# The end of a two-block transformer kernel: squares and statistic of one token half moved one step ahead, one activation table for both roots, three residual pairs added by TensorE

## The reference, cut to what matters

```python
    h2 = _rmsnorm(x, g_mlp_pre[l])
    ff = jnp.einsum('bsf,fd->bsd',
                    jnp.square(jax.nn.relu(jnp.einsum('bsd,df->bsf', h2, w_up[l]))), w_down[l])
    x = x + _rmsnorm(ff, g_mlp_post[l])
```

## Time and profile before

| | us |
|---|---|
| median of 3 runs | 2459.04 (2458.66 to 2460.85) |
| the profiled execution | 2458.39 |
| its span | 2456.7 |
| TensorE busy | 2421.7 (99%) |
| VectorE busy | 1678.2 (68%) |
| ScalarE busy | 1050.0 (43%) |
| last product of step 27 begins | 2432.38 |
| last addition on VectorE ends | 2452.87 |

### The profile page before, as it was taken

One profiled execution on the slowest core, in us unless ns is written; L12 is line 12 of the kernel. 1 busy time (PEld: TensorE's weight loads), 2 busy tenths in 40 slices (PEclk: granted clock), 3 DMA queues, 4 the chain that ended last, 5 costly groups with the idle time before them and its releaser, 6 DMA issues.

```text
span 2456.7 us, 29766 instructions
## 1 busy us (share of the span) xinstructions
PE 2421.7 (99%) x11558; PEld 1928.9 (79%) x11558; DVE 1678.2 (68%) x1992; ACT 1050.0 (43%) x1503; POOL 139.1 (6%) x227
## 2 busy tenths in 40 slices
PE   8999999999999999999999999999999999999997
PEld 6887766688888888888788777788878888888885
DVE  5238776646877778698873655455588877786888
ACT  5225676634433333333642333333356333334336
POOL 1002100000000010000001000000001000100001
PEclk9999999999999999999999999999999999999999
DMA  6110000142433381500134122233445533715103
GB/s 222 50 43 22 2 1 1 53 146 103 155 123 109 103 308 65 209 1 18 53 108 142 43 81 72 72 134 135 143 150 176 172 103 105 262 45 196 45 1 137
DMA packets 76245, 252.22 MB, mean 103 GB/s; under 512 B 6320, under 2 KB 6368, under 8 KB 76080
## 3 DMA queue, kind: packets, MB, share of 16 engines
q1 hardware_dynamic: 43792, 131.08, 16.7%
q0 software_dynamic: 32320, 119.32, 13.0%
HBM read 186.78 MB, written 62.91 MB: 102 GB/s over the span
## 4 chain that ended last, share of the span: by engine, by line
PE 79%; DVE 8%; ACT 2%; issue 2%; DVEq 0%; ACTq 0%
PE ps L2720 24%; PE ps L3133 20%; PE ps L3171 18%; PE ps L3301 6%; PE ps L3004 2%; PE ps L3066 1%; DVE opQ_lo L2135 1%; DVE opQ_lo L2132 1%; PE ps L3046 1%; DVE spot L2177 1%; DVE ql_raw L2172 1%; PE ps L3228 1%; PE ps L3247 1%; PE ps L2968 1%; PE ps L3237 1%
## 5 line engine op out<-in xcount | busy, mean ns | idle before, releaser
L3171 PE MATMUL ps<-opQ_hi 128*128 128x512 f32 x896 | 350.3, 391 | 2.8 <-DVE opQ_lo L2135 2.8
L3171 PE MATMUL ps<-opQ_lo,opQ_hi 128*128 128x512 f32 x896 | 348.8, 389 | 0.0
L3171 PE MATMUL ps<-opQ_hi,opQ_lo 128*128 128x512 f32 x896 | 348.7, 389 | 0.0
L3171 PEld LDWEIGHTS ps<-opQ_hi 128*128 128x128 f32 x896 | 168.2, 188 | 42.1 <-DVE opQ_lo L2135 7.1
L2720 PE MATMUL ps<-opP_hi,w_hi 128*128 128x512 f32 x638 | 199.0, 393 | 2.1 <-DVE T L2419 0.7
L2720 PE MATMUL ps<-opP_lo,w_hi 128*128 128x512 f32 x638 | 196.6, 389 | 0.0
L2720 PE MATMUL ps<-opP_hi,w_lo 128*128 128x512 f32 x638 | 196.4, 389 | 0.0
L3171 PEld LDWEIGHTS ps<-opQ_hi,opQ_lo 128*128 128x128 f32 x896 | 168.2, 188 | 35.2
L3171 PEld LDWEIGHTS ps<-opQ_lo,opQ_hi 128*128 128x128 f32 x896 | 168.2, 188 | 34.6 <-issue 0.2
L1275 ACT ACTIVATE opQ_hi<-spot 128x1024 fp32r<-128x1024 f32 x80 | 84.9, 1061 | 235.8 <-PE ps L3171 196.7
L885 ACT ACTIVATE w_hi<-w_stage 128x1024 fp32r<-128x1024 f32 x104 | 109.3, 1051 | 174.1 <-PE ps L2720 145.7
(11 more groups left out here) (444 smaller groups left out, 4750.9 us busy)
## 6 DMA issues: line engine op xcount, KB each, us to landing
w_stage<-in_w_stream SPq DMA_DIRECT2D x104, 512.0 KB, 3.7
h_spill<-T POOLq DMA_DIRECT2D x56, 512.0 KB, 5.3
pair_raw<-in_w_stream SPq DMA_DIRECT2D x26, 1024.0 KB, 5.8
spot<-in_w_stream SPq DMA_DIRECT2D x24, 1024.0 KB, 7.1
spot<-h_spill POOLq DMA_DIRECT2D x24, 1024.0 KB, 9.5
qh_raw<-in_w_stream SPq DMA_DIRECT2D x8, 1024.0 KB, 11.1
ql_raw<-h_spill POOLq DMA_DIRECT2D x8, 1024.0 KB, 7.5
g_spill<-T POOLq DMA_DIRECT2D x16, 512.0 KB, 2.9
```

The lines of the kernel that those rows point to most:

```text
L3171: mm = pe.matmul(ps[:, down_bank(sc, f) + m, :], weight, operand, start=(g == 0 and kt == 0 and weight is wh and operand is hi), stop=(g = ...
```

## The change

On four engines the order at the end is written anew.

- VectorE and ScalarE: the squares of half 1 and their sums (`end_square`, `end_add`) of tiles 0 to 5 now follow the folds of step 25, ahead of the parts of step 26; tiles 6 and 7 follow those parts. Before, tiles 0 to 3 (VectorE) or 0 to 4 (ScalarE) followed the parts of step 26 and the others those of step 27.
- TensorE: the statistic of half 1 is taken in the middle of step 26 instead of step 27.
- ScalarE: behind the squares of tiles 6 and 7 one table set with both the logarithm and the exponential is loaded (`preload_act_table_set`); the four loads at the roots are gone. Three gains of half 1 come ahead of step 27's parts. The root of half 1 comes behind six gains, ahead of the squares of half 0, and all four squares' gains of half 0 come ahead of the last folds.
- The residual of pair 0 of half 0 is also added by TensorE (`TURNED_PAIRS`): three turned pairs instead of two. The first tile of the first of them now stands ahead of the four squares' products of half 0 on TensorE. All three copies by ScalarE come at its very end, and all three stores go by GpSimd; SyncE stores the other three pairs of half 0.
- VectorE: the scales and the residual additions are two functions now; three scales of half 1 come ahead of the last folds.

```diff
+TURNED_PAIRS = ((1, 0), (1, 1), (0, 0))
...
-            for j in range(3):
-                sp.wait_ge(n4["added"], 2 * DT + 2 + j + 1)
+            for j in range(1, 3):
+                sp.wait_ge(n4["added"], 2 * DT + 2 + j)
                 sp.dma_start(out_pair(0, j), end_pair(X, 0, j)).then_inc(y_stored, 16)
...
-            for j in range(2):
-                pool.wait_ge(n4["ln"], 3 + j + 1)
-                pool.dma_start(out_pair(1, j), end_pair(X, 1, j)).then_inc(ya_stored, 16)
-            pool.wait_ge(ya_stored, 16 * 4)
+            for i, (h, j) in enumerate(TURNED_PAIRS):
+                pool.wait_ge(n4["ln"], 3 + i + 1)
+                pool.dma_start(out_pair(h, j), end_pair(X, h, j)).then_inc(ya_stored, 16)
+            pool.wait_ge(ya_stored, 16 * 5)
...
-                        if sc == 1 and i == 26:
-                            if x == 0:
-                                gate_square(0)
-                                gate_square(1)
-                            else:
-                                for o in range(5):
-                                    end_square(1, o)
+                        if sc == 1 and i == 26 and x == 0:
+                            gate_square(0)
+                            gate_square(1)
+                        if sc == 1 and i == 25 and x == 1:
+                            for o in range(6):
+                                end_square(1, o)
+                        if sc == 1 and i == 26 and x == 1:
+                            end_square(1, 6)
+                            end_square(1, 7)
+                            act.preload_act_table_set("natural_log_exp_and_others")
+                            for o in range(3):
+                                end_gain(1, o)
...
-            for o in range(5, DT):
-                end_square(1, o)
-            for o in range(5):
-                end_gain(1, o)
+            for o in range(3, 6):
+                end_gain(1, o)
+            half_root(n4, 2, 0, end_r[1])
+            for o in range(6, DT):
+                end_gain(1, o)
             for o in range(4):
                 end_square(0, o)
-            half_root(n4, 2, 0, end_r[1])
+            for o in range(4):
+                end_gain(0, o)
             for o in range(4, DT):
                 end_square(0, o)
-            for o in range(5, DT):
-                end_gain(1, o)
             half_root(n5, 2, 1, end_r[0])
-            for o in range(DT):
+            for o in range(4, DT):
                 end_gain(0, o)
-                if o in (1, 5):
-                    pair_out(o // 4)
+            for i in range(3):
+                pair_out(i)
...
+                        if sc and x == 1 and i == 25:
+                            for o in range(6):
+                                end_add(1, o)
                         if sc and i == 26:
                             down_turn(x)
...
-                    for o in range(4):
+                    for o in range(6, DT):
                         end_add(1, o)
...
-            for o in range(4, DT):
-                end_add(1, o)
...
+            end_scale(1, 0)
+            end_scale(1, 1)
             for o in range(4):
                 end_add(0, o)
+            end_scale(1, 2)
             for o in range(4):
                 last_fold(1, o)
-            for j in range(4):
-                end_scale(1, j)
-            for j in range(4):
+            end_scale(1, 3)
+            end_residual(1, 2)
+            end_residual(1, 3)
+            end_scale(0, 0)
+            for j in range(1, 4):
                 end_scale(0, j)
+                end_residual(0, j)
...
-                            if x == 1 and sc == 1 and i == STEPS - 1 and kt == 1:
+                            if x == 1 and sc == 1 and i == STEPS - 2 and kt == 1:
                                 pe.wait_ge(ff["down"], vec_no(1, 1, "F5b"))
                                 half_statistic(n4, 2, 0, mix_sum)
...
+            def turned(i, x):
+
+                h, j = TURNED_PAIRS[i]
+                n = 2 * (2 * (j % 2) + x) + j // 2
+                pe.wait_ge(n4["scaled"], 2 * DT + 4 * (1 - h) + j + 1)
+                pe.wait_ge(tile_landed[n], END_BACK[n])
+                for tiles in (X, Xend):
+                    mm = pe.matmul(ps[:, 2 + 2 * i + x, :], ident[:, :], end_pair(tiles, h, j)[:, x],
+                                   start=(tiles is X), stop=(tiles is Xend))
+                return mm
+
+            turned(0, 0)
             for o in range(4, DT):
                 pe.wait_ge(n5["sq"], 2 * DT + o + 1)
                 mm = pe.matmul(ps[:, 1, :], ones[:, :], end_sq[(o - 1) % 4], start=False, stop=(o == DT - 1))
             mm.then_inc(n5["stat"], 1)
...
+            turned(0, 1).then_inc(n4["stat"], 1)
+            pe.wait_ge(ff["down"], vec_no(1, 1, "F4_3"))
+            for i in range(1, 3):
+                turned(i, 0)
+                turned(i, 1).then_inc(n4["stat"], 1)
```

More of the change, by code:

```diff
@@ L1350, in end_square, with end_gain @@
                 act.activation(dst, X[:, 2 * m + a, cols_of(h)], ACT.Square).then_inc(norm["sq"], 1)
+            def end_gain(h, o):
+                a, m = o // 4, o % 4
+                n = 2 * m + a
+                act.wait_ge((n5, n4)[h]["sq"], 16 + o + 1)
+                act.activation(X[:, n, cols_of(h)], X[:, n, cols_of(h)], ACT.Copy, scale=col[:, C_MLPPOST + n:C_MLPPOST + n + 1])                   .then_inc(n5["hi"], 1)
             for n in range(FF_PLAIN[0]):
@@ L1580, in _, with pair_out @@
             down_act(1)
[L1582 to L1592 removed]
+            def pair_out(i):
+                h, j = TURNED_PAIRS[i]
+                act.wait_ge(n4["stat"], 3 + i + 1)
+                act.activation(end_pair(X, h, j), banks(2 + 2 * i, 2).rearrange("p (m t) -> p m t", t=HALF), ACT.Copy)\
                    .then_inc(n4["ln"], 1)
[L1595 to L1597 removed]
+            for o in range(3, 6):
+                end_gain(1, o)
+            half_root(n4, 2, 0, end_r[1])
+            for o in range(6, DT):
                 end_gain(1, o)
@@ L2682, in end_scale, with end_residual @@
                     v.wait_ge((n5, n4)[h]["r"], 3)
[L2683 removed]
                 v.wait_ge(n5["hi"], 16 + 8 * (1 - h) + 2 * j + 2)
                 v.tensor_tensor(end_pair(X, h, j), end_pair(X, h, j), bc(end_r[h].unsqueeze(1), [P, 2, HALF]), ALU.mult)                 .then_inc(n4["scaled"], 1)
+            def end_residual(h, j):
+                a, m0 = j // 2, 2 * (j % 2)
                 v.wait_ge(n4["scaled"], 2 * DT + 4 * (1 - h) + j + 1)
[L2687 to L2698 removed]
+                for m in range(m0, m0 + 2):
+                    v.wait_ge(tile_landed[2 * m + a], END_BACK[2 * m + a])
+                if h == 0 and j == 3:
+                    for x in range(2):
+                        v.tensor_tensor(end_pair(X, h, j)[:, x], end_pair(X, h, j)[:, x], end_pair(Xend, h, j)[:, x], ALU.add)\
+                         .then_inc(n4["added"], 1)
+                else:
+                    v.tensor_tensor(end_pair(X, h, j), end_pair(X, h, j), end_pair(Xend, h, j), ALU.add).then_inc(n4["added"], 1)
+            end_scale(1, 0)
+            end_scale(1, 1)
             for o in range(4):
                 end_add(0, o)
+            end_scale(1, 2)
             for o in range(4):
                 last_fold(1, o)
[L2703 to L2705 removed]
+            end_scale(1, 3)
[3 more added lines that the diff above has]
+            for j in range(1, 4):
                 end_scale(0, j)
+                end_residual(0, j)
         @block.tensor
@@ L3330, in _ @@
             mm.then_inc(n5["stat"], 1)
-            for j in range(2):
-                a, m0 = j // 2, 2 * (j % 2)
-                pe.wait_ge(n4["scaled"], 2 * DT + j + 1)
-                for x in range(2):
-                    n = 2 * (m0 + x) + a
-                    pe.wait_ge(tile_landed[n], END_BACK[n])
-                    for tiles in (X, Xend):
-                        mm = pe.matmul(ps[:, 2 + 2 * j + x, :], ident[:, :], end_pair(tiles, 1, j)[:, x],
-                                       start=(tiles is X), stop=(tiles is Xend))
-                mm.then_inc(n4["stat"], 1)
+            turned(0, 1).then_inc(n4["stat"], 1)
[3 more added lines that the diff above has]
+                turned(i, 1).then_inc(n4["stat"], 1)
 def _layout(i):
```

25 lines of the change are left out of this document (4 added, 21 removed).

## The result

| | before | after |
|---|---|---|
| median of 10 runs each, us | 2459.3 (2458.4 to 2460.85) | 2466.27 (2465.28 to 2468.87) |
| profiled execution, us | 2458.39 | 2468.5 |
| its span, us | 2456.7 | 2466.8 |
| TensorE busy, us | 2421.7 | 2429.4 |

The ratio is 1.0031 (95% interval 1.0022 to 1.0039): slower, by 7.0 us. 2462.9 was forecast and 2464.9 was the top of the range, so the forecast was wrong.

What follows compares the result with a forecast made beforehand. TensorE was taken to bound the kernel up to the last product, then stores and VectorE ending almost together. Stores 2.35 us (wait included) plus clock 1.5 made 3.85 on the 2459.04 median: 2462.9 us, range 2458.8 to 2464.9.

Steps and rivals of the forecast that it cites:

- TensorE's wait on them: At step 26, TensorE waits 3.2 us for low parts that VectorE makes behind five additions.
- step 27 late a second time: At step 27, no second delay: VectorE's low parts are ready with 1.6 us of slack.
- wait and restart together: At step 26, the 3.2 us wait plus 0.2 us for TensorE's restart delays what follows by 3.4 us.
- half clock behind the wait: On TensorE after step 26's wait, the clock falls to half, costing 1.5 us; given two in three.
- Part 4: At the final stores: data flow starts later, so stores fall silent 2.35 us later, and the end with them.
- What bounds the kernel now: Opening account: TensorE up to the last product, then stores and VectorE together; stores silent 2.1 us before the span's end.
- the stores' new queue: At the final stores: their new queue costs nothing beyond the 2.35 us delay.
- two signs of being wrong: TensorE meets step 26 without a wait, or DMA engines run dry before the last store is issued.
- A: The forecast itself: wait at step 26, half clock, stores at the end; 2462.9 us, chance 0.50.
- B: At step 26 the wait comes but the clock holds: +2.35, 2461.4 us; chance 0.25.
- C: At the end the stores drain slowly, 1.6 us on top of A: 2464.6 us; chance 0.13.
- D: The additions find room, the wait at step 26 stays under 1 us: -1.1 us, 2458.0 us; chance 0.12.

Runs made afterwards that it cites:

- e3: The changed kernel, with 13 unused 128x128 products on TensorE during its wait for step 26's low parts; 2466.92 us over 8 runs, ratio 1.0027.
- e5: The kernel before, with the last pair's two stores issued by GpSimd instead of SyncE; 2465.45 us, ratio 1.0022.
- e8: The kernel before, with only the second turned pair's store moved from GpSimd to SyncE; 2459.46 us, ratio 0.9995.
- e10: e3, with all three turned pairs stored by SyncE instead of GpSimd; 2460.08 us, ratio 1.0003.
- g2: The kernel before, with one table load for both roots and one scale of half 1 ahead of the last folds; 2459.71 us, ratio 0.9999.
- e7: The changed kernel with two turned pairs; pair 0 of half 0 gets its residual from VectorE and its store from SyncE; 2463.5 us, ratio 1.0013.
- e1: The changed kernel, with the third turned pair's store issued by SyncE instead of GpSimd; 2462.82 us, ratio 1.0013.
- e4: The changed kernel, with squares, sums and statistic of half 1 put back where they were before; 2463.05 us, ratio 1.0013.
- e6: The kernel before, with one table load for both roots instead of the four loads at the roots; 2460.83 us, ratio 1.0002.
- g3: g2, with both turned pairs stored by SyncE instead of GpSimd; 2457.99 us, ratio 0.9991.
- e2: The changed kernel, without GpSimd's wait for its stores at its end; SyncE still waits for all; 2463.74 us, ratio 1.0018.
- e9: g2, without GpSimd's wait for its stores at its end; SyncE still waits for all; 2457.42 us, ratio 0.9991.

## Why the prediction was wrong

Its sum, step by step, in the time scale of before (after's times less 2.43; the predicted times are those with the half clock):

| step | predicted | measured |
|---|---|---|
| low parts of step 26 end | 2424.03 | 2424.05 |
| TensorE's wait on them | 3.2 | 3.12 |
| step 27 late a second time | no | no |
| wait and restart together | 3.4 | 3.43 (e3) |
| half clock behind the wait | two in three, 1.5 | yes, 1.57 (e3) |
| root of half 0 ready | 2445.2 | 2445.17 |
| VectorE's last addition ends | 2453.7 | 2453.68 |
| store of the first turned pair issued | 2448.85 | 2448.83 |
| stores silent, later by | 3.85 | 3.82 |
| span ends, later by | 3.85 | 7.67 |

**The step that failed** is the last of Part 4. "What bounds the kernel now" put silence "2.1 us ahead of the end of the span", and Part 4 carried "the end with it": the 2.1 us were taken for a constant that follows the last byte. They were no constant. They were the remainder of another path, GpSimd's: last store issued at 34.08, landed 3.7 later, 5.4 more to the end. Part 4 also said "the stores' new queue ... cost nothing beyond that", and that was the edit that mattered: with the third turned pair GpSimd's last store is the last one issued in the whole kernel, at 40.22, landed in 5.1. It is 6.14 us later by issue and 1.4 by landing, 7.5 together, and the end moved by 7.67. e5 made a loss of 4.70 us of this kind in the kernel before; e8 and e10 took GpSimd's share away. "Stores and VectorE end almost together; neither alone has slack" was wrong with it: both had 1.3 us of slack behind GpSimd, and g2, with VectorE 1.75 us earlier, gained 0.12.

The working had the material for a doubt. It never asked which row ends the span, and took the first thing that stopped 2.1 us ahead of it. Neither of its two signs of being wrong (no wait at step 26, engines that run dry) came. The chain that ended last of the kernel before doesn't help, for it has no store in its end, which lies 3.8 us ahead of the span's:

```profile
2451.58 0.69 DVE X L2692
2452.27 0.60 DVEq L161
```

A column of GpSimd's and SyncE's last landings, and the wait of 1.5 us at L161 on an engine that had long been done, would have shown that someone else came last.

**The rivals.** A (0.50) is what happened up to the silence, with every time in the table within 0.1 us. B fell: the clock did not hold. C (0.13) comes nearest in size, 2464.6, but its mechanism did not come: from 2453 to 2460 the DMA share is 1.00 at 371 GB/s, against 376 in before. D (0.12) fell: the wait came in full. No rival had a separate path to the end, so the range stopped 1.4 us short, and slower by over 0.2% got 0.17. The change was judged right where it was expected to hurt and missed where it was thought to be free.

The other claim of Part 4, that the data of later stores are ready before the engines are free, held: the DMA share is 1.00 from 2453 to 2460. That is also why turning a third pair could not gain: e7 has it back on VectorE, and its stores are silent sooner.

## What to carry to other kernels

Between the last byte and the end of the span find out which engine the program waits for, before a store is moved: list each queue's last store with its landing, and see which one the end follows. In this kernel a store at the end belongs to SyncE, and GpSimd should get none late nor wait for its own where another engine already waits for all. When a helper's additions are moved ahead of what TensorE needs, count the wait once as time and once as clock; if it can't be avoided, some small products in it can keep the clock, as 13 did here.

## What the runs showed of the hardware

- **GpSimd's stores hold the end.** In nine kernels of nine where GpSimd waits for its stores and theirs is the later path, the span ends 5.4 to 5.7 us behind its last landing (before, after, e1, e3, e4, e5, e6, e7, g2). In the three where GpSimd waits but SyncE's side is later (e8, g3, e10) the end is some 0.4 us behind SyncE's last landing. Without GpSimd's wait 2.7 us (e2) or 2.2 us (e9) go; e2 still ends 2.9 us behind its landing and 8.0 behind its issue, e9 0.4 behind SyncE's last landing. What the engine does in these microseconds is open.
- **The row of a GpSimd store is not its transfer.** It shows 0.7 us busy; the landing took 3.2 us with free DMA engines and up to 5.8 us where stores piled up (e4). The Trainium skill, "Perfetto Trace Analysis", section "DMA Instruction — SWDGE (GPSIMD)", says that such a row ends when the descriptors are made and not when the data have moved; the trace agrees (0.71 beside 5.1 us).
- **The clock's price.** A wait of 3.12 us in dense products was followed by 3.4 us at a granted clock of 0.50, which cost 1.57 us, and 13 products of 128x128 in the wait kept the clock at 1.00 (e3).
- **A table load costs its row.** Two loads of 1.28 us taken away moved the root by 2.47 us (e6), with no further stop beside them.
